# Summing the squares of two layer-norm halves on GpSimd, with one matmul per half on PE, issued one unit later

## The reference

```python
def layer_norm(x, g, b):
    mu = jnp.mean(xf, -1, keepdims=True)
    var = jnp.mean(jnp.square(xf - mu), -1, keepdims=True)
    return ((xf - mu) * lax.rsqrt(var + EPS) * g + b)
...
    x = layer_norm(ALPHA * x + gt1 * y, ln1_g[l], ln1_b[l])
    h = x * (1.0 + sc2) + sh2
    f = jnp.square(jax.nn.relu(h @ w_ff1[l])) @ w_ff2[l]
    x = layer_norm(ALPHA * x + gt2 * f, ln2_g[l], ln2_b[l])
```

## Time and profile before

| | us |
|---|---|
| median of 3 runs | 2549.51 (2548.55 to 2551.8) |
| the profiled execution | 2552.21 |
| its span in the trace | 2550.4 |
| busy in it: PE | 2400.7 (94%) |
| busy: DVE | 1395.5 (55%) |
| busy: POOL | 729.4 (29%) |
| busy: ACT | 630.2 (25%) |

### The profile page before, as it was taken

The page is one execution under the profiler, slowest core; times in us unless marked ns, Lnnn a source line. Parts: engine busy times, 40 slices in busy tenths (PEclk is TensorE's granted clock), DMA queues, the critical chain, the costliest instruction groups (busy, mean ns, idle before and its releaser), DMA issues.

```text
span 2550.4 us, 28694 instructions
## 1 busy us (share of the span) xinstructions
PE 2400.7 (94%) x11308; PEld 1901.5 (75%) x11308; DVE 1395.5 (55%) x1621; ACT 630.2 (25%) x948; POOL 729.4 (29%) x492
## 2 busy tenths in 40 slices
PE   6999889999899999999998799999998999999998
PEld 3776656667678888888875488885586788879976
DVE  7567754435633554455446789996428321337733
ACT  4012344422512101100124611214214200024410
POOL 1231330035463332333265011210046223340021
PEclk9999889999999999999999899999999999999999
DMA  6652000122242332333232021113232531110021
GB/s 229 204 178 72 21 19 9 46 87 83 58 124 75 103 104 88 90 105 98 87 112 74 9 104 42 35 31 120 75 116 83 164 86 46 49 41 10 1 91 74
DMA packets 228850, 206.94 MB, mean 81 GB/s; under 512 B 15248, under 2 KB 203280, under 8 KB 227712
## 3 DMA queue, kind: packets, MB, share of 16 engines
q1 hardware_dynamic: 223552, 178.61, 23.4%
q10 hardware_dynamic: 3840, 21.89, 2.2%
q0 software_dynamic: 1344, 4.91, 0.5%
HBM read 180.35 MB, written 17.83 MB: 78 GB/s over the span
## 4 chain that ended last, share of the span: by engine, by line
PE 79%; DVE 8%; issue 3%; ACT 3%; PEld 2%; DMA 2%; POOL 1%; PEldq 1%; SPq 0%; ACTq 0%; DVEq 0%; POOLq 0%
PE G L1671 28%; PE G L306 26%; PE M L3063 3%; PE M L309 2%; PE G L1159 2%; PE G L2560 2%; PE M L1706 1%; PE G L2376 1%; PE M L2376 1%; PE G L2403 1%; PE M L1110 1%; PE M L2562 1%; PE M L3040 1%; PE G L2317 1%; PEldq L3229 1%
## 5 line engine op out<-in xcount | busy, mean ns | idle before, releaser
L280 POOL TENSOR_SCALAR WH<-RAW 128x1024 fp32r<-128x1024 f32 (+1 forms) x156 | 134.2, 860 | 885.1 <-PE G L1671 465.0
L306 PE MATMUL G<-HH,WH 128*128 128x512 f32 x1056 | 333.6, 397 | 13.2 <-DVE HL L489 4.0
L306 PE MATMUL G<-HL,WH 128*128 128x512 f32 x1056 | 329.0, 393 | 0.0
L306 PE MATMUL G<-HH,WL 128*128 128x512 f32 x1056 | 328.1, 392 | 0.0
L283 POOL TENSOR_TENSOR WL<-RAW,WH 128x1024 fp32r<-128x1024 f32 (+1 forms) x156 | 301.1, 1930 | 13.0
L1671 PE MATMUL G<-HH,WH 128*128 128x512 f32 x624 | 216.5, 397 | 15.8 <-POOL WL L283 5.9
L306 PEld LDWEIGHTS G<-HH,WH 128*128 128x128 f32 x1056 | 189.8, 189 | 55.6 <-issue 13.5
L306 PEld LDWEIGHTS G<-HL,WH 128*128 128x128 f32 x1056 | 190.4, 189 | 37.6
L306 PEld LDWEIGHTS G<-HH,WL 128*128 128x128 f32 x1056 | 190.1, 189 | 37.7
L1671 PE MATMUL G<-HL,WH 128*128 128x512 f32 x624 | 213.3, 392 | 0.0
L1671 PE MATMUL G<-HH,WL 128*128 128x512 f32 x624 | 213.3, 392 | 0.0
(11 more groups left out here) (548 smaller groups left out, 4390.6 us busy)
## 6 DMA issues: line engine op xcount, KB each, us to landing
RAW<-in_w_ff SPq DMA_DIRECT2D x40, 512.0 KB, 4.1
RAW<-in_w_ff SPq DMA_DIRECT2D x80, 256.0 KB, 2.8
WVEC<-in_w_ada SPq DMA_DIRECT2D x24, 512.0 KB, 4.7
FVEC<-in_e_w_mod SPq DMA_DIRECT2D x24, 512.0 KB, 3.9
FVEC<-in_o_w_mod SPq DMA_DIRECT2D x24, 512.0 KB, 4.0
RAW<-in_o_w_in SPq DMA_DIRECT2D x24, 512.0 KB, 3.7
RAW<-in_e_w_in SPq DMA_DIRECT2D x20, 512.0 KB, 3.7
ADA<-in_w_ada SPq DMA_DIRECT2D x4, 2048.0 KB, 18.4
```

Source lines behind the costliest of these rows:

```text
L280: pool.tensor_scalar(hi, raw, 1.0, 0.0, ALU.mult, ALU.add).then_inc(w_high, 1)
L306: m = pe.matmul(G[s][:, n * w:(n + 1) * w], part[s][:, k, :], acts[i][:, k, n * w:(n + 1) * w], start=first, stop=last)
```

## The change

Two of the four halves are changed, the second half of l1 and the first half of l2. Their eight squares are added by POOL, seven adds into SQSUM (the first 512 columns of ER), right behind the split of the weights of unit ("a", 0, 3, 0) for l1 and ("a", LAST, 3, 1) for l2. PE sums SQSUM alone, with one matmul (two records), and does so behind that same unit, where the eight matmuls stood one unit earlier. The squares' buffers are now let go by POOL's adds. For l1, ACT's root and DVE's inverse are moved behind the feed of that unit; for l2 they already stood there.

```diff
+        SQSUM = ER[:, 0:512]
+        POOLED = {("a", 0, 3, 0): ("l1", 1), ("a", LAST, 3, 1): ("l2", 0)}
...
                 split_one(pool, r0 + i, wf_U(i), 4 if kind == "b" else 8)
+                if WF[i] in POOLED:
+                    tag, h = POOLED[WF[i]]
+                    sq = HSQ2 if tag == "l2" else HSQ
+                    for k in range(1, KT):
+                        g = KT * h + k
+                        pool.wait_ge(S(tag + "_sq"), g + 1)
+                        if k > 1:
+                            pool.wait_ge(S(tag + "_squ"), g)
+                        pool.tensor_tensor(SQSUM, sq[0][:] if k == 1 else SQSUM, sq[k % 2][:], ALU.add)\
+                            .then_inc(S(tag + "_squ"), 2 if k == 1 else 1)
...
+        def pooled_var_pe(pe, tag, h):
+            pe.wait_ge(S(tag + "_squ"), KT * h + KT)
+            pe.matmul(M[1][:, half(h)], ONES[:], SQSUM, start=True, stop=True).then_inc(S(tag + "_var"), 1)
...
-                     ("a", 0, 0, 0): lambda: norm_mean_pe(pe, "l1", 1), ("a", 0, 2, 0): lambda: norm_var_pe(pe, "l1", 1),
+                     ("a", 0, 0, 0): lambda: norm_mean_pe(pe, "l1", 1), ("a", 0, 3, 0): lambda: pooled_var_pe(pe, "l1", 1),
...
-                     ("a", LAST, 2, 1): lambda: norm_var_pe(pe, "l2", 0),
+                     ("a", LAST, 3, 1): lambda: pooled_var_pe(pe, "l2", 0),
...
             def root(tag, h):
-                act.wait_ge(S(tag + "_squ"), KT * h + KT)
+                if (tag, h) in POOLED.values():
+                    act.wait_ge(S(tag + "_var"), 1)
+                else:
+                    act.wait_ge(S(tag + "_squ"), KT * h + KT)
...
             feed(("a", 0, 2, 0))
+            feed(("a", 0, 3, 0))
             root("l1", 1)
-            feed(("a", 0, 3, 0))
             first_finish(1)
...
                 feed_low(("a", 0, j, 0))
+            feed_low(("a", 0, 3, 0))
             inverse("l1", 1)
-            feed_low(("a", 0, 3, 0))
```

## The result

The changed kernel takes 2559.39 us (median of 7; 2558.11 to 2563.38) against 2551.25 us for the kernel before on the same chips: a ratio of 1.0037, 95% interval 1.0026 to 1.0047. It is slower, by 8.1 us by the medians and by 9.4 us by the ratio; the forecast was slower by 5.9. The sign was right, and so was what holds PE up. The size was too small, by about a third. Most of the missing part lies in two terms of the sum: what the clock costs behind a gap, and the part that was to come back behind the moved reciprocal, which did not.

The account below looks back on a forecast made before the run. PE's matmuls were taken to bound the kernel wherever PE is never late. l1: 1.7 + 3.3 - 0.8 = 4.2 us; l2: 1.7 us; in all +5.9 us, forecast 2555.4 us, range 2551.5 to 2560.

Parts of the forecast that it names:

- The bound and the holder: Both places: PE's next unit waits for ACT's Relu behind the squares, PE standing still over 7 us.
- The adds and the hand-overs: POOL's adds of 1.28 us, 0.08 us between them, pace the squares; at l1 the Relu comes 0.4 us late.
- The estimate of 1.12 us an add: POOL's adds by the skill's table: both Relus 0.8 us sooner, the sum 4.3 us.
- The clock: Held-up unit behind PE's idle 7 us, both places: 6.93 us instead of 5.63, 1.3 us more.
- the term 3.3: l1: root and reciprocal behind the unit's feed make Relu to first scaled tile 5.97 us, 3.3 us more.
- a part comes back: l1, behind the first scaled tile: DVE's HL takes 0.69 us instead of 1.51, POOL's split being done; 0.8 us gained.
- the dearer adds: Rival, both places: adds at 1.61 us delay each Relu by 1.7 more; +9.3 us, chance 0.23 shared with second clock loss.
- The saving: Rival: accumulator free at 668.9, PE runs the next unit under the adds at both places; -7 us, chance 0.07.
- The clock did not hold: Against the rival that PE keeps full clock behind the gaps at both places; +2.7 us, chance 0.17.
- The "b" row: Rival at l1: the "b" units catch up, bound by PE, 1.8 us back; +4.1 us, chance 0.18.
- A second fall of the clock at l1: Rival: PE waits over 3 us for the first eviction after two "b" units; +7.5 us, chance 0.23 shared with dearer adds.
- the fourth rival: It costs more: adds at 1.61 us (+9.3 us) or a second clock loss at l1 (+7.5 us); chance 0.23.

Follow-up runs that it names:

- relu_first: The changed kernel with ACT's feed of the second "a" unit ahead of the eight squares at both places; ratio 0.9992.
- its control: The kernel before with ACT's feed of the second "a" unit moved ahead of the squares, the eight sums still on PE; ratio 1.0002.
- the early eviction: DVE evicts ("b", 0, 0, 0) ahead of the first scaled tile, each "b" unit one step sooner; alone on the kernel before, ratio 0.9998.
- order_only: The kernel before with only l1's root on ACT and reciprocal on DVE moved behind the feed of ("a", 0, 3, 0); ratio 1.0024.
- after_evict: The changed kernel with the early eviction; ratio 1.0028.
- evict_only: The kernel before with the early eviction alone; ratio 0.9998.
- dve_adds: The changed kernel with the seven adds on DVE, none on POOL, and ACT's feed ahead of the squares; ratio 0.9975.
- filler, again: The changed kernel with eight throwaway sums on PE in each of the two gaps before the held-up unit, second measurement; ratio 1.0033.
- order_evict: The kernel before with l1's root and reciprocal behind the feed of ("a", 0, 3, 0), and the early eviction; ratio 1.0011.

## Why the prediction was partly wrong, by its own steps

- **The bound and the holder: right.** PE waits 7.43 us for the Relu behind the squares ("over 7 us" forecast). relu_first against its control shows it.
- **The adds and the hand-overs: right.** From the mark, the first add starts where the forecast had it (670.20 - 2.66 = 667.54; 667.5), the Relu comes 0.54 us late (0.4 forecast), and an add takes 1.29 us (1.28). The estimate of 1.12 us an add, from the table of the Trainium skill, "GPSIMD Engine Reference", section "3.1 Elementwise — side-by-side cycle accounting", is not what the trace has. The advice of that page of the Trainium skill, section "4.1 Engine selection", to give such adds to VectorE agrees with the runs: with the Relu first in both, the ratio is 0.9992 with the adds on POOL and 0.9975 on DVE.
- **The clock: right in kind, short in size.** I took one fall of 1.6 us at each place, from the row of 649.94. From Relu to Relu the unit cost 1.76 us more at l1 (8.54 against 6.78) where 1.3 was forecast, and 2.40 us at l2 (9.19 against 6.79). A gap of 7.4 us was followed by more time at half clock, 4.5 and 5.8 us, than one of 4.6 (3.4 us, by a mean granted clock of 0.76 from 649.94 to 657.10). That is 1.6 us of the miss; the Relus, each 0.15 us later than forecast, are another 0.3.
- **The order at l1: the term 3.3 right, the term behind it wrong. This is the step that failed.** From that unit's Relu to the first scaled tile it is 5.98 us (5.97 forecast). But "a part comes back", -0.8, was wrong in sign: from the first tile to ("a", 0, 0, 1) it takes 0.36 us more than before. Its reason was that POOL would have its split behind it. POOL's splits came later too, as PE had been held up: the subtraction of 694.78 is still under way, and the HL of 695.21 takes 1.38 us, where 0.69 was forecast. And the term left out that PE runs dry a second time, for 3.98 us, as DVE's first eviction stands behind the reciprocal; at 701.93 DVE in turn waits 1.61 us for that late unit. I saw the wait for the first eviction and put it, at 1.6 us, among the rivals with the dearer adds, at 0.23. It was no chance: the gap of 3.9 to 4.0 us stands in five of the six traces in which the reciprocal follows the fourth feed without the early eviction; in the sixth, relu_first, PE had stood before the sum instead. order_only shows the price of this step alone: ratio 1.0024 where 1.0010 was forecast.
- **The sum.** l1: 0.54 (Relu) + 1.76 (clock) + 3.34 (order) + 0.36 = 6.0 us, against 4.2. l2, from its own sum of the means (1347.88; 1339.34 before): 0.56 + 2.40 = 3.0, against 1.7. In all 9.0 by the trace, 8.1 by the medians and 9.4 by the ratio, against 5.9.
- **The rivals.** The saving did not arrive, and could not. The clock did not hold. The "b" row did not catch up. A second fall of the clock at l1, half of the fourth rival, is what happened, at 7.5 us forecast; its other half, adds at 1.61 us, did not.

The place where I should have looked longer is the step by which I let the 0.8 us come back: I followed DVE's queue up to its next instruction and not PE's accumulators, both of which are full while DVE does its reciprocal.

## What to carry to other kernels

Work taken off the busiest engine gains only if that engine can go on: ask which buffer the next unit needs, who frees it, and what stands ahead of that instruction on its engine. Moving a step behind another moves the cover of all that follows it; walk on to the point where each accumulator of the busy engine is read. And put the adds where the idle engine is fast enough for the pace of the buffers: here two square buffers made the adder's pace that of everything behind.

## What the runs showed of the hardware

- A gap of 3.9 to 4.0 us on PE was followed by half clock in all six places with one here (mean granted clock over the next 5 us 0.50 to 0.69), and one of 7.4 us by 4.5 and 5.8 us of work at half.
- Behind smaller gaps the length alone doesn't tell. Ahead of ("a", 0, 0, 1) the clock stayed at 1.00 behind gaps of 2.09 (the change), 2.38 (before), 3.08 (after_evict) and 3.38 us (evict_only), and fell to 0.66 over 5 us behind 2.10 (order_only), 2.14 (dve_adds), 2.27 (filler, again) and 3.09 us (order_evict). Such a fall cost 1.4 to 1.7 us, and order_only has three. So an edit can cost or gain several us at gaps that it does not touch.
- 14 us of throwaway matmuls on the busiest engine cost no measurable time, in two measurements, as they filled gaps.
